# RWKV scan: four operands turned by 128x128 transposes for two chunks at a time, in place of 64x64 products with an identity

## The chip, the cores and the metric

One Trainium2 chip, and one of its cores. The time is the device time of one launch, in microseconds (us). Weights, inputs and constants lie in device memory; the kernel brings them in itself.

## The reference, cut to what matters

The program runs two transformer blocks after each other on 512 tokens of width 1024. The change lies in the second block, in its RWKV mixer, between the projections that make r, k, v, a, b and the output of the mixer:

```python
def rwkv7_scan(r, w, k, v, a, b):
    ...
    def step(state, inp):
        r_t, w_t, k_t, v_t, a_t, b_t = inp
        sa = jnp.einsum('bhvk,bhk->bhv', state, a_t)
        state = state * w_t[:, :, None, :] + sa[..., None] * b_t[:, :, None, :] + v_t[..., None] * k_t[:, :, None, :]
        return state, jnp.einsum('bhvk,bhk->bhv', state, r_t)
```

There are 16 heads of 64 features. The kernel does the recurrence in chunks of 64 tokens: within a chunk all 64 steps are written as products of 64x64 matrices per head, and a 64x64 state per head goes from chunk to chunk. All data is fp32.

## The kernel before, in words

The engines run their own programs, in the order in which a list of stages is built; semaphores tie them together. The stage of interest is `RwkvScan`. Ahead of it `RwkvInputs` makes the scaled operands r, k (`kx`), v, a (`aa`) and b (`bb`), each with the features on the partitions: tile p of 8 holds head 2p on partitions 0 to 63 and head 2p+1 on 64 to 127, and 512 tokens along the free axis. After it comes `SplitTiles` "gate_input", which splits the normalised input `xn` into a high and a low part (ScalarE writes `gate_input_hi`, GpSimd writes `gate_input_lo`), then `RwkvOutput` (norm, bonus, gate of the mixer), then `Gated` (projections).

`RwkvScan` goes over 8 chunks (`NCH`), c = 0 to 7, with a lead-in c = -1. In each turn of the loop the work of chunk c ("now") is woven with the first half of chunk c+1 ("next"): x, b_ra, d2, d2t, d4, d2_dm, d8, m2, m3 are "next", the others are "now". Each step is one `product`: 16 matmuls of 64x64 by 64x64, two per tile p, one for each head, with one PSUM bank as output; y has three such terms and z two. A `twin` (k_ra, b_ra, d2_dm) is 16 matmuls with 128 columns and fills two banks. The bonus is one full 128x128 matmul with 512 columns. Four products a chunk have the identity on the right: vn, bn, an, kn turn v, b, a and k of the chunk, so that tokens lie on the partitions; they are read as left factors by q, y and z (vn), z (bn, kn) and wt (an). (mn and mn2 use the identity too; the change leaves them.)

Each step takes the next of five PSUM banks in the order of the table `PERIOD`; a step can begin when the step five places before it has been drained (`open_aux`). TensorE signals `aux_full`; ScalarE copies most steps to SBUF (`copy`, L1994), VectorE drains the others: masks, sums (`summed`, L2046), the sum of sa (L2096) and of the state z (L2102, L2105), the bonus (L2080). Both work through their steps in program order. `state_ready` counts the state's updates, and `wait_end` waits for the last.

While RwkvInputs worked, the room of `xn` held its temporaries. `Move` "xn_back" brings `xn` back from device memory: one transfer of 2 MB that GpSimd issues (L2423), and for which `SplitTiles` "gate_input" waits on ScalarE (L514). On ScalarE the eight instructions of gate_input_hi stand before the squares of RwkvOutput (L2171):

```python
        load_xn = Move(k, "xn_back", xn, xn_dram, [inp.wait_scaled])
        scan = RwkvScan(k, inp, sbuf, ra)
        begin_gated = Begin(k)
        xs6 = SplitTiles(k, "gate_input", xn, view_r("gate_input_hi", 0, [DT_, S]),
                         view_r("gate_input_lo", 24576, [DT_, S]),
                         lambda e, j: (scan.wait_end(e), load_xn.wait_done(e)), alone=True)
        outp = RwkvOutput(k, scan, zg, inp.zg_ready, rr, vv, aa, kk,
                          view(30272, [DT_, S]))
```

Of the kernel before, what the change touches and what calls it, by code (L numbers as in the profile page):

```python
# [23 lines left out]
ACT = mybir.ActivationFunctionType  # L24
# [3 lines left out]
P = 128  # L28
S = 512
D = 1024  # L30
DT_ = D // P
# [1814 lines left out]
class RwkvScan(Stage):  # L1846
# [3 lines left out]

    PERIOD = (("next", "x"), ("now", "vn"), ("now", "k_ra0"), ("now", "k_ra1"), ("now", "mn"), ("now", "g"),
              ("next", "b_ra0"), ("next", "b_ra1"), ("now", "m4"), ("next", "d2"), ("next", "d2t"), ("now", "bn"),
              ("now", "g2"), ("now", "mn2"), ("next", "d4"), ("now", "an"), ("now", "bonus"), ("next", "d2_dm0"), ("next", "d2_dm1"),
              ("now", "m5"), ("now", "q"), ("next", "d8"), ("next", "m2"), ("now", "wt"), ("now", "u"), ("now", "kn"),
              ("now", "sa"), ("next", "m3"), ("now", "y"), ("now", "z"))

    def __init__(self, k, prep, buf, ra):

        super().__init__(k)
        self.prep, self.buf, self.ra = prep, buf, ra
        self.t = [{} for _ in range(NCH)]
        for c in range(-1, NCH):
            for which, step in self.PERIOD:
                at = c if which == "now" else c + 1
                if 0 <= at < NCH:
                    self.t[at][step] = k.take_aux()
        self.state_ready = k.sem("scan_state_ready")
        self.one_plus_d = k.sem("scan_one_plus_d_ready")  # L1870
        self.rkk_ready = k.sem("scan_rkk_ready")

    def chunk(self, ap, c):
        return ap[:, :, c * CH:(c + 1) * CH]

    def tensor(self, pe):
        k, b = self.k, self.buf
# [20 lines left out]
        def twin(t, name, lhs, rhs):  # L1898

            for half in range(2):  # L1900
# [6 lines left out]
                        mm = pe.matmul(out[part, p - 4 * half], lhs[part, p, :], rhs(p)[part], start=True, stop=True)  # L1907
                mm.then_inc(k.aux_full, 1)

        def drained(t, *steps):  # L1910

            for step in steps:
                k.wait_aux_drained(pe, t[step])

        for c in range(-1, NCH):
            n = c + 1
            now, nxt = c >= 0, n < NCH
            if now:
                t = self.t[c]
                ac, bc, kc, rc, vc = (self.chunk(x, c) for x in (aa, bb, kx, r, v))  # L1920
                x32, x64, rbt = b["x32"][c % 2], b["x64"][c % 2], b["rbt"][c % 2]
                ra = lambda p, c=c: self.ra[:, :, p * S + c * CH:p * S + (c + 1) * CH]
            if nxt:
                tn = self.t[n]
                an_, bn_ = self.chunk(aa, n), self.chunk(bb, n)
                ra_n = lambda p, n=n: self.ra[:, :, p * S + n * CH:p * S + (n + 1) * CH]
                product(tn["x"], (an_, bn_))
            if now:
                product(t["vn"], (vc, None))
                twin(t, "k_ra", kc, ra)  # L1930
                drained(t, "m3")
                product(t["mn"], (b["ml1"], None))
                product(t["g"], (x32, b["ml1"]))
            if nxt:
                twin(tn, "b_ra", bn_, ra_n)
            if now:
                drained(t, "mn", "g")
                product(t["m4"], (b["mn"], b["g"]))
            if nxt:
                drained(tn, "x", "b_ra0", "b_ra1")  # L1940
                product(tn["d2"], (b["dt"], b["d"]))
                product(tn["d2t"], (b["d"], b["dt"]))
            if now:
                product(t["bn"], (bc, None))
# [12 lines left out]
            if nxt:  # L1957
                pe.wait_ge(self.one_plus_d, n + 1)
                twin(tn, "d2_dm", b["d2"], lambda p: b["d2t_me0"][:, :, p, :])
            if now:  # L1960
                drained(t, "mn2", "g2")
                product(t["m5"], (b["mn"], b["g"]))
                drained(t, "k_ra0", "k_ra1", "vn")
                product(t["q"], (b["akt"], b["vn"]))
            if nxt:
                drained(tn, "d4", "d2_dm0", "d2_dm1")
                product(tn["d8"], (b["d4t"], b["d4"]))
                product(tn["m2"], (b["d4"], b["me1"]))
            if now:
                drained(t, "an", "m5")  # L1970
                product(t["wt"], (b["an"], b["ml1"]))
                drained(t, "q")
                product(t["u"], (b["ml1"], b["q"]))
                product(t["kn"], (kc, None))
                drained(t, "wt")
                pe.wait_ge(self.state_ready, c + 1)
                product(t["sa"], (b["wt"], b["z"]))
            if nxt:
                drained(tn, "d8", "m2")
                product(tn["m3"], (b["d8"], b["me0"]))  # L1980
            if now:
                drained(t, "sa")
                product(t["y"], (b["z"], rc), (b["sa"], rbt), (b["vn"], b["rkt"]))
                drained(t, "bn", "kn")
                product(t["z"], (b["bn"], b["sa"]), (b["kn"], b["vn"]))

    def scalar(self, act):


        k, b = self.k, self.buf  # L1990

        def copy(t, dst):
            k.wait_aux_full(act, t)
            act.activation(dst, k.aux(t).rearrange("p (a b) -> p a b", b=CH), ACT.Copy).then_inc(  # L1994
                k.aux_drained[t % NX], 1)

        for c in range(-1, NCH):
            now, nxt = c >= 0, c + 1 < NCH
            if now:
                t = self.t[c]  # L2000
                copy(t["vn"], b["vn"])
                copy(t["mn"], b["mn"])
                copy(t["g"], b["g"])
            if nxt:
                tn = self.t[c + 1]
                copy(tn["d2"], b["d2"])
                copy(tn["d2t"], b["d2t"])
            if now:
                copy(t["bn"], b["bn"])
                copy(t["g2"], b["g"])  # L2010
                copy(t["mn2"], b["mn"])
            if nxt:
                copy(tn["d4"], b["d4"])
            if now:
                copy(t["an"], b["an"])
                copy(t["q"], b["q"])
            if nxt:
                copy(tn["d8"], b["d8"])
            if now:
                copy(t["wt"], b["wt"])  # L2020
                copy(t["u"], b["u"])
                copy(t["kn"], b["kn"])
                copy(t["y"], self.chunk(self.prep.rkv[0], c))

    def vector(self, dve):
# [22 lines left out]
        for c in range(-1, NCH):  # L2048
# [430 lines left out]
def build(nc, x, consts, vecs, weights, bucket, rel, rel_last, mem, lora_in, out):  # L2479
    with ExitStack() as ctx:  # L2480
# [131 lines left out]
        for at, (name, n) in zip((38464, 38472, 38480, 38488, 38496), (("w0h", 8), ("a0h", 8), ("kah", 8), ("kac", 8), ("mu1", 27))):  # L2612
# [8 lines left out]
        names = ("x32", "x32", "x64", "x64", "rbt", "rbt", "d2", "d4", "d2t", "me0", "me1", "ml0", "ml1", "an", "q",  # L2621
                 "akt", "mn", "g", "vn", "bn", "kn", "rkt", "rkk", "d", "dt")
        sbuf = dict(zip(names, place))
        for i, n in enumerate(("x32", "x64", "rbt")):
            sbuf[n] = place[2 * i:2 * i + 2]
        for n, shared in (("d8", "d"), ("d4t", "dt"), ("wt", "akt"), ("u", "mn"), ("sa", "g")):
            sbuf[n] = sbuf[shared]
        sbuf["z"] = view(28672, [DT_, CH])
# [285 lines left out]
```

## Time and profile before

| what | value |
|---|---|
| time, median of 3 runs | 2407.27 us (2407.03 to 2411.24) |
| profiled execution, its own time | 2410.71 us |
| its span in the profile | 2408.8 us |
| TensorE matmul busy | 2217.2 us, 92% of the span |
| VectorE / ScalarE / GpSimd busy | 1043.4 / 870.9 / 333.1 us |
| matmuls of `product` (L1894), first and last start | 823.6 to 1081.6 us |

The profile is of one execution. Times in it count from the start of the span; "PE" is TensorE's matmuls, "PEld" its weight loads, DVE VectorE, ACT ScalarE, POOL GpSimd. The trace has two records for each fp32 matmul, so a product of 16 matmuls is "x32"; a transpose has one. The profiled execution's own time is 1.9 us above its span, and 3.4 us above the median of the runs.

### The profile page before, as it was taken

The numbers are of one execution on the slowest core, as the hardware profiler recorded it, in microseconds if no ns is written. First come the engines' busy times: TensorE is split into PE (matmuls) and PEld (weight loads), VectorE is DVE, ScalarE is ACT, GpSimd is POOL, SyncE is SP. The second block draws the span as 40 slices with busy tenths as digits, with TensorE's granted clock in tenths as the row PEclk, the third lists the DMA queues.
The fourth block names the chain that finished last, engine by engine and source line by source line (L and its number), as shares of the span: only waits on it lengthen the run. The fifth ranks groups of instructions, "written<-read, shape, count | busy, mean of one in ns | idle before, by whom it ended". The sixth has DMA issues, their size and how long they took to land.

```text
span 2408.8 us, 37512 instructions
## 1 busy us (share of the span) xinstructions
PE 2217.2 (92%) x16140; PEld 1682.4 (70%) x16140; DVE 1043.4 (43%) x1684; ACT 870.9 (36%) x1442; POOL 333.1 (14%) x395
## 2 busy tenths in 40 slices
PE   6988999999699899997999899979998787999999
PEld 3856788888366699992776664548776555888887
DVE  3144544343535544437334345563333444555522
ACT  3253333232445333334235136652243433333221
POOL 1443000001104200002000016660101012000000
PEclk8998999999899999997998799999998898999999
DMA  3212222232222200000253330002422101222222
GB/s 133 68 45 70 88 96 88 96 97 96 106 74 77 79 4 4 4 4 29 88 143 124 117 96 19 1 8 91 147 84 91 53 27 61 92 92 96 93 95 85
DMA packets 47411, 178.20 MB, mean 74 GB/s; under 512 B 5343, under 2 KB 5855, under 8 KB 46352
## 3 DMA queue, kind: packets, MB, share of 16 engines
q1 hardware_dynamic: 43056, 154.12, 19.4%
q0 software_dynamic: 4192, 21.70, 2.9%
q8 instruction: 128, 2.10, 0.4%
q14 instruction: 35, 0.29, 0.0%
HBM read 166.30 MB, written 10.55 MB: 73 GB/s over the span
## 4 chain that ended last, share of the span: by engine, by line
PE 82%; DVE 8%; ACT 5%; issue 3%; POOL 1%; DMA 1%; SPq 0%; DVEq 0%; ACTq 0%; POOLq 0%
PE ps L289 18%; PE ps L290 18%; PE ps L294 17%; PE ps L1894 8%; PE ps L474 4%; PE ps L1141 2%; PE ps L891 2%; PE ps L1907 2%; DVE arena L427 2%; PE ps L875 1%; PE ps L463 1%; PE ps L844 1%; ACT arena L986 1%; PE ps L408 1%; DVE arena L947 1%
## 5 line engine op out<-in xcount | busy, mean ns | idle before, releaser
L275 DVE TENSOR_TENSOR w_lo<-wring,w_hi 128x1024 fp32r<-128x1024 f32 (+1 forms) x243 | 301.9, 1244 | 340.1 <-ACT w_hi L269 340.1
L269 ACT ACTIVATE w_hi<-wring 128x1024 fp32r<-128x1024 f32 (+1 forms) x243 | 253.7, 1044 | 445.3 <-PE ps L294 430.9
L289 PE MATMUL ps<-ffn_input_hi,w_hi 128*128 128x512 f32 x352 | 141.8, 403 | 10.7 <-ACT ffn_input_hi L514 8.7
L290 PE MATMUL ps<-ffn_input_hi,w_lo 128*128 128x512 f32 x352 | 140.7, 400 | 0.0
L1894 PE MATMUL ps<-arena 64*64 64x64 f32 x4096 | 135.2, 218 | 5.3 <-issue 4.4
L1994 ACT ACTIVATE arena<-ps 128x512 f32<-128x512 f32 x120 | 71.7, 597 | 177.0 <-PE ps L1894 177.0
L1894 PEld LDWEIGHTS ps<-arena 64*64 64x64 f32 x4096 | 129.8, 135 | 7.4 <-issue 5.8
L1033 POOL TENSOR_TENSOR arena<-arena 128x512 f32<-128x512 f32 (+3 forms) x160 | 111.4, 721 | 39.2 <-DVE arena L939 34.2
L289 PE MATMUL ps<-mlp_input_hi,w_hi 128*128 128x512 f32 x256 | 102.9, 402 | 9.4 <-ACT mlp_input_hi L514 8.6
L641 DVE TENSOR_TENSOR arena<-arena,ps 128x512 f32<-128x512 f32 x56 | 38.5, 688 | 153.6 <-PE ps L294 153.6
L290 PE MATMUL ps<-mlp_input_hi,w_lo 128*128 128x512 f32 x256 | 102.1, 399 | 0.0
L289 PE MATMUL ps<-mlp_hi,w_hi 128*128 128x512 f32 x256 | 101.2, 395 | 0.0
L290 PE MATMUL ps<-mlp_hi,w_lo 128*128 128x512 f32 x256 | 101.2, 395 | 0.0
L986 ACT ACTIVATE arena<-arena 128x512 f32<-128x512 f32 (+3 forms) x160 | 88.2, 552 | 29.3 <-DVE arena L931 29.2
L289 PE MATMUL ps<-mixer_input_hi,w_hi 128*128 128x512 f32 (+1 forms) x216 | 90.6, 419 | 7.2 <-ACT mixer_input_hi L514 7.2
L474 PEld LDWEIGHTS ps<-wring,arena 128*128 128x128 f32 x832 | 96.0, 196 | 1.1 <-issue 1.0
L474 PE MATMUL ps<-wring,arena 128*128 128x128 f32 (+1 forms) x832 | 96.0, 279 | 0.0
L418 POOL TENSOR_TENSOR square<-square 128x512 f32<-128x512 f32 x21 | 36.4, 1735 | 412.2 <-ACT square L390 412.2
L294 PE MATMUL ps<-ffn_input_lo,w_hi 128*128 128x512 f32 x352 | 90.0, 397 | 0.1
L289 PEld LDWEIGHTS ps<-ffn_input_hi,w_hi 128*128 128x128 f32 x352 | 67.1, 191 | 30.9 <-issue 11.0
L289 PE MATMUL ps<-gate_input_hi,w_hi 128*128 128x512 f32 x192 | 79.7, 415 | 8.8 <-DVE w_lo L275 7.3
L290 PE MATMUL ps<-mixer_input_hi,w_lo 128*128 128x512 f32 (+1 forms) x216 | 87.6, 406 | 0.0
(358 smaller groups left out, 4545.1 us busy)
## 6 DMA issues: line engine op xcount, KB each, us to landing
wring<-weights SPq DMA_DIRECT2D x276, 512.0 KB, 3.3
bias_wide_scratch<-bias_line_scratch POOLq DMA_DIRECT2D x1, 4096.0 KB, 25.9
arena<-bias_wide_scratch POOLq DMA_DIRECT2D x1, 4096.0 KB, 16.9
wring<-weights SPq DMA_DIRECT2D x8, 384.0 KB, 3.0
arena<-x_t SPq DMA_DIRECT2D x1, 2048.0 KB, 7.7
x_scratch<-arena POOLq DMA_DIRECT2D x1, 2048.0 KB, 7.8
xn_scratch<-arena POOLq DMA_DIRECT2D x1, 2048.0 KB, 6.5
arena<-xn_scratch POOLq DMA_DIRECT2D x1, 2048.0 KB, 9.0
```

What stands on the lines that cost most here:

```text
L269: act.activation(self.w_hi[:, m % SPLIT, 0:n], self.wring[:, g % RING, 0:n], ACT.Copy).then_inc(self.w_hi_ready, 1)
L275: dve.tensor_tensor(self.w_lo[:, m % SPLIT, 0:n], self.wring[:, g % RING, 0:n], self.w_hi[:, m % SPLIT, 0:n].bitcast(F32), ALU.subtract).t ...
L289: pe.matmul(out, hi[:, c, :], src.hi[:, at + c, :], start=(at + c == 0), stop=False)
L290: pe.matmul(out, lo[:, c, :], src.hi[:, at + c, :], start=False, stop=False)
L294: mm = pe.matmul(out, hi[:, c, :], src.lo[:, at + c, :], start=False, stop=(last and c == kc - 1))
L427: dve.scalar_tensor_tensor(self.dst[:, j, :], self.src[:, j, :], k.vec(self.gain, j), r, ALU.mult, ALU.mult).then_inc(k.xn_ready, 1)
L474: mm = pe.matmul(k.acc(t)[:, b * self.m:(b + 1) * self.m], self.src(c)[:, b * P:(b + 1) * P], w[:, c, :], start=(c == 0), stop=(c == total ...
L891: mm = pe.matmul(out[e * HD:(e + 1) * HD, j * P:S], h.values(j, e), self.b.pt[e][:, COL[j]:COL[j] + S - j * P], start=(h.first and h.compr ...
L986: ins = act.activation(seg, seg, ACT.Exp, bias=b.negmax[:, u % 2, c], scale=-1.0, accum_out=b.sum[:, u % 2, c])
L1033: pool.tensor_tensor(seg, seg, inv[:, e:e + 1].to_broadcast([P, P * (i + 1)]), ALU.mult).then_inc(self.scaled, 1)
L1894: mm = pe.matmul(cut(out, p, e), cut(lhs, p, e), right, start=(i == 0), stop=(i == len(terms) - 1))
L1994: act.activation(dst, k.aux(t).rearrange("p (a b) -> p a b", b=CH), ACT.Copy).then_inc(k.aux_drained[t % NX], 1)
```

## The change

`turn` transposes v, b, k or a with `pe.transpose`: tile p of two chunks is 128 features by 128 tokens and is turned in one 128x128 transpose, so that chunk c comes to lie on partitions 0 to 63 and chunk c+1 on 64 to 127. Four tiles fill a bank, so a turn is 8 transposes and two banks (T0, T1). `turns` says for how many chunks a turn in chunk c is: v and b are turned in chunks 0, 2, 4, 6, for two chunks each; k and a in chunks 1, 3, 5 for two, and in chunks 0 and 7 for one (then 64 tokens wide). In the other chunks nothing is turned. That is 14 turns for two chunks and 4 for one.

The result has to be moved so that head 2p+e lies on partitions 64e to 64e+63. `turned` does that by copies of 64 partitions by 256 elements, two for each chunk and bank: ScalarE takes both banks of v and the first of b, a and k; VectorE the second of b, a and k. Each operand has two buffers by chunk parity. They lie in the room of `xn` (from 4096), so `xn_back` now waits for the end of the scan too.

```diff
+    def turns(self, name, c):
+        if name in "vb":
+            return (0, 2)[c % 2 == 0]
+        return 1 if c in (0, NCH - 1) else (0, 2)[c % 2]
+
+    def turned(self, eng, copy, name, c, half):
+        k = self.k
+        if self.turns(name, c):
+            t = self.t[c][f"{name}T{half}"]
+            k.wait_aux_full(eng, t)
+            for h in range(self.turns(name, c)):
+                x = k.aux(t)[h * CH:(h + 1) * CH, :].rearrange("p (a e b) -> p a e b", e=2, b=HD)
+                for e in range(2):
+                    dst = self.buf[f"{name}n"][(c + h) % 2][e * CH:(e + 1) * CH, 4 * half:4 * half + 4, :]
+                    ins = copy(dst, x[:, :, e, :])
+            ins.then_inc(k.aux_drained[t % NX], 1)
...
+        def turn(name, x, c):
+            width = CH * self.turns(name, c)
+            for half in range(2 if width else 0):
+                bank = self.t[c][f"{name}T{half}"]
+                k.open_aux(pe, bank)
+                for p in range(4):
+                    mm = pe.transpose(k.aux(bank)[0:width, p * P:(p + 1) * P],
+                                      x[:, 4 * half + p, c * CH:c * CH + width], k.const("ident"))
+                mm.then_inc(k.aux_full, 1)
...
-                product(t["vn"], (vc, None))
+                turn("v", v, c)
...
-                product(t["bn"], (bc, None))
+                turn("b", bb, c)
...
-                product(t["an"], (ac, None))
+                turn("a", aa, c)
...
-                product(t["kn"], (kc, None))
+                turn("k", kx, c)
...
-                copy(t["vn"], b["vn"])
+                self.turned(act, move, "v", c, 0)
+                self.turned(act, move, "v", c, 1)
...
-                copy(t["kn"], b["kn"])
+                self.turned(act, move, "k", c, 0)
...
                 summed(t["m4"], "ml0", "ml1", t["m3"])
+                self.turned(dve, dve.tensor_copy, "b", c, 1)
                 self.weigh(dve, c)
-                k.wait_aux_drained(dve, t["vn"])
+                self.turned(dve, dve.tensor_copy, "a", c, 1)
+                self.wait_turned(dve, "v", c)
...
             if now:
+                self.turned(dve, dve.tensor_copy, "k", c, 1)
                 k.wait_aux_drained(dve, t["u"])
                 k.wait_aux_full(dve, t["sa"])
...
-        load_xn = Move(k, "xn_back", xn, xn_dram, [inp.wait_scaled])
         scan = RwkvScan(k, inp, sbuf, ra)
+        load_xn = Move(k, "xn_back", xn, xn_dram, [inp.wait_scaled, scan.wait_end])
```

TensorE, before, in chunk 1 from d2 and d2t (the first row) on; rows with `consts_sb` and 64x64 are bn, mn2, an and kn, L1955 is the bonus, L1907 the twin d2_dm:

```order
L1894 MATMUL ps<-square 64x64 x32
L1894 MATMUL ps<-consts_sb,arena 64x64 x16
L1894 MATMUL ps<-arena 64x64 x16
L1894 MATMUL ps<-consts_sb,arena 64x64 x16
L1894 MATMUL ps<-arena 64x64 x16
L1894 MATMUL ps<-consts_sb,arena 64x64 x16
L1955 MATMUL ps<-arena,consts_sb 128x512
L1907 MATMUL ps<-arena 64x128 x16
L1894 MATMUL ps<-arena 64x64 x32
L1894 MATMUL ps<-arena,square 64x64 x16
L1894 MATMUL ps<-arena 64x64 x48
L1894 MATMUL ps<-consts_sb,arena 64x64 x16
```

TensorE now, in the same chunk, from m4, d2, d2t and g2 (the first row) on; L1942 are the transposes, of a and then of k:

```order
L1919 MATMUL ps<-arena 64x64 x64
L1919 MATMUL ps<-consts_sb,arena 64x64 x16
L1919 MATMUL ps<-arena 64x64 x16
L1942 MATMUL ps<-consts_sb,arena 128x128 x8
L1992 MATMUL ps<-arena,consts_sb 128x512
L1932 MATMUL ps<-arena 64x128 x16
L1919 MATMUL ps<-arena 64x64 x96
L1942 MATMUL ps<-consts_sb,arena 128x128 x8
L1919 MATMUL ps<-arena 64x64 x128
```

The turn of b between d2t and g2 is gone from this odd chunk; a, for two chunks, stands right ahead of the bonus, and k between u and sa.

VectorE, before, in chunk 1: the end of d2_dm (L2087), the sums of m5 and m2 (L2046), of sa (L2096), of m3, and the state:

```order
L2087 TENSOR_TENSOR arena<-arena,ps 128x256
L2046 TENSOR_TENSOR arena<-arena,ps 128x512 [waits aux_full,aux_drained4]
L2046 TENSOR_TENSOR arena<-arena,ps 128x512 [waits aux_full,aux_drained4,aux_drained3]
L2096 TENSOR_TENSOR arena<-arena,ps 128x512 [waits aux_full,aux_drained0]
L2046 TENSOR_TENSOR arena<-arena,ps 128x512 [waits aux_full,aux_drained3]
L2102 TENSOR_TENSOR arena<-arena,ps 128x512 [waits scan_state_ready,aux_full]
```

VectorE now, at the same place:

```order
L2131 TENSOR_TENSOR arena<-arena,ps 128x256
L2088 TENSOR_TENSOR arena<-arena,ps 128x512 [waits aux_full,aux_drained2]
L2088 TENSOR_TENSOR arena<-arena,ps 128x512 [waits aux_full,aux_drained2,aux_drained1]
L1892 COPY arena<-ps 64x256 [waits aux_full]
L1892 COPY arena<-ps 64x256 x3
L2141 TENSOR_TENSOR arena<-arena,ps 128x512 [waits aux_full,aux_drained3]
L2088 TENSOR_TENSOR arena<-arena,ps 128x512 [waits aux_full,aux_drained1]
L2147 TENSOR_TENSOR arena<-arena,ps 128x512 [waits scan_state_ready,aux_full]
```

Four copies of k now stand between the sum of m2 and the sum of sa.

GpSimd, around the scan (L1841 and L1843 are the last work of RwkvInputs, L1325 belongs to a later stage), as a difference, with the semaphores waited for:

```order
 L1841 TENSOR_TENSOR arena<-arena 128x512 [waits kk_a_ready]
 L1843 TENSOR_TENSOR arena<-arena 128x512 [waits acc_drained2]
-L2423 DMA arena<-xn_scratch 128x4096 [waits bkr_scaled_ready,a_scaled_ready]
+L2468 DMA arena<-xn_scratch 128x4096 [waits scan_state_ready,bkr_scaled_ready,a_scaled_ready]
 L518 TENSOR_TENSOR gate_input_lo<-arena,gate_input_hi 128x512 [waits gate_input_hi_ready] x8
-L1325 DMA arena<-rel_bias 32x16 [waits aux_drained4]
+L1325 DMA arena<-rel_bias 32x16 [waits aux_drained3]
```

The order is the same; the transfer has one more semaphore to wait for, that of the scan's state.

## Rows read from the trace of the kernel before

**Rows 1.** The page's first line

```profile
span 2408.8 us, 37512 instructions
```

**Rows 2.** Windows: the scan's middle; busy us (records) by engine, PEclk the granted clock

```profile
855.00:1050.00 195.00, 194.28 (x5782) 188.08 (x5783) 84.84 (x163) 58.55 (x99) 0.00 (x0) 1.00 0.02 4
```

**Rows 3.** Timeline in chunk 1: start, us, engine, line, xcount

```profile
880.71 1.13 PE L1894 MATMUL ps<-consts_sb,arena 64*64 64x64 f32 x32
881.64 1.13 PE L1894 MATMUL ps<-arena 64*64 64x64 f32 x32
...
884.44 1.13 PE L1894 MATMUL ps<-consts_sb,arena 64*64 64x64 f32 x32
885.50 1.12 PE L1955 MATMUL ps<-arena,consts_sb 128*128 128x512 f32 x2
886.56 1.96 PE L1907 MATMUL ps<-arena 64*64 64x128 f32 x32
```

**Rows 4.** Chain that ended last, behind the scan: a full fp32 matmul of 512 columns

```profile
1093.60 0.86 PE ps L2155 x2
```

**Rows 5.** Timeline of TensorE in the attention: transposes (L875) between 64-row products

```profile
1486.61 0.88 PE L875 MATMUL ps<-consts_sb,arena 128*128 128x128 f32 x6
1487.41 0.70 PE L844 MATMUL ps<-arena 64*128 64x256 f32 x4
```

**Rows 6.** Transposes: duration ns min/median/max; then a run of eight (start, us)

```profile
L875 PE MATMUL ps<-consts_sb,arena x400: 272/273/332, 147.5 to 1603.6; 128*128 128x128 f32 x134
1933.64 1.09 PE L2253 MATMUL ps<-consts_sb,arena 128*128 128x128 f32 x8 [2.31 <-DVE arena L2285]
```

**Rows 7.** Timeline of TensorE in the last chunk: m4, bn, g2

```profile
1063.91 1.15 PE L1894 MATMUL ps<-arena 64*64 64x64 f32 x32 [0.73 <-issue]
1064.87 1.13 PE L1894 MATMUL ps<-consts_sb,arena 64*64 64x64 f32 x32
1065.91 1.15 PE L1894 MATMUL ps<-arena 64*64 64x64 f32 x32
```

**Rows 8.** Groups by form: copies out of PSUM; busy us, mean ns

```profile
L1159 ACT ACTIVATE arena<-ps 128x256 f32<-128x256 f32 x8 | 3.1, 384 | 19.7 <-PE ps L1141 19.3
L1000 ACT ACTIVATE arena<-ps 64x512 f32<-64x512 f32 x8 | 4.6, 574 | 0.0
L2086 DVE COPY square<-ps 128x256 f32<-128x256 f32 x16 | 6.8, 424 | 7.2 <-PE ps L1907 6.8
```

**Rows 9.** Timeline in chunk 1, second half: sa, m3 (their weight loads), sum of sa, y

```profile
894.83 1.02 PEld L1894 LDWEIGHTS ps<-arena 64*64 64x64 f32 x32
895.76 1.02 PEld L1894 LDWEIGHTS ps<-arena,square 64*64 64x64 f32 x32
896.11 0.69 DVE L2096 TENSOR_TENSOR arena<-arena,ps 128x512 f32<-128x512 f32 x1 [3.02 <-PE ps L1894]
896.85 5.72 PEld L1894 LDWEIGHTS ps<-arena 64*64 64x64 f32 x190
```

**Rows 10.** DMA issues: KB each, median us from issue to landing

```profile
arena<-x_t SPq DMA_DIRECT2D x1, 2048.0 KB, 7.7
arena<-xn_scratch POOLq DMA_DIRECT2D x1, 2048.0 KB, 9.0
arena<-mem_t POOLq DMA_DIRECT2D x1, 1024.0 KB, 11.8
```

**Rows 11.** Timeline at the end of the scan

```profile
1083.30 4.27 ACT L514 ACTIVATE gate_input_hi<-arena 128x512 fp32r<-128x512 f32 x8 [1.77 <-DVE arena L2105]
1087.47 1.13 ACT L2171 ACTIVATE square<-arena 128x512 f32<-128x512 f32 x2
1088.23 1.63 PE L2155 MATMUL ps<-square,consts_sb 128*128 128x512 f32 x2 [4.50 <-ACT square L2171]
```

**Rows 12.** Windows: clock in the attention, and just behind the scan (columns as in group 2)

```profile
1479.70:1500.00 20.30, 18.95 (x131) 10.36 (x130) 12.24 (x54) 13.56 (x43) 13.54 (x26) 1.00 0.00 1
1089.00:1091.00 2.00, 2.00 (x4) 0.80 (x3) 0.69 (x1) 0.00 (x0) 2.00 (x3) 0.50 0.00 0
```

More of the change, by code:

```diff
@@ L1846 @@
 class RwkvScan(Stage):
[L1853 to L1856, printed above, removed]
+    PERIOD = (("next", "x"), ("now", "vT0"), ("now", "vT1"), ("now", "k_ra0"), ("now", "k_ra1"), ("now", "mn"), ("now", "g"),
+              ("next", "b_ra0"), ("next", "b_ra1"), ("now", "m4"), ("next", "d2"), ("next", "d2t"), ("now", "bT0"), ("now", "bT1"),
+              ("now", "g2"), ("now", "mn2"), ("next", "d4"), ("now", "aT0"), ("now", "aT1"), ("now", "bonus"), ("next", "d2_dm0"), ("next", "d2_dm1"),
+              ("now", "m5"), ("now", "q"), ("next", "d8"), ("next", "m2"), ("now", "wt"), ("now", "u"), ("now", "kT0"), ("now", "kT1"),
               ("now", "sa"), ("next", "m3"), ("now", "y"), ("now", "z"))
@@ L1866, in __init__ @@
                 at = c if which == "now" else c + 1
-                if 0 <= at < NCH:
+                if 0 <= at < NCH and (step[1:2] != "T" or self.turns(step[0], at)):
                     self.t[at][step] = k.take_aux()
@@ L1874, in chunk, with wait_turned @@
         return ap[:, :, c * CH:(c + 1) * CH]
+    def turns(self, name, c):
[13 more added lines that the diff above has]
+            ins.then_inc(k.aux_drained[t % NX], 1)
+    def wait_turned(self, eng, name, c):
+        start = next(i for i in range(c, -1, -1) if self.turns(name, i))
+        for half in range(2):
+            self.k.wait_aux_drained(eng, self.t[start][f"{name}T{half}"])
     def tensor(self, pe):
@@ L1919, in tensor @@
                 t = self.t[c]
-                ac, bc, kc, rc, vc = (self.chunk(x, c) for x in (aa, bb, kx, r, v))
+                kc, rc = self.chunk(kx, c), self.chunk(r, c)
+                vn, bn, kn, an = (b[f"{name}n"][c % 2] for name in "vbka")
                 x32, x64, rbt = b["x32"][c % 2], b["x64"][c % 2], b["rbt"][c % 2]
@@ L1962, in tensor @@
                 product(t["m5"], (b["mn"], b["g"]))
-                drained(t, "k_ra0", "k_ra1", "vn")
-                product(t["q"], (b["akt"], b["vn"]))
+                drained(t, "k_ra0", "k_ra1")
+                self.wait_turned(pe, "v", c)
+                product(t["q"], (b["akt"], vn))
             if nxt:
@@ L1969, in tensor @@
             if now:
-                drained(t, "an", "m5")
-                product(t["wt"], (b["an"], b["ml1"]))
+                drained(t, "m5")
+                self.wait_turned(pe, "a", c)
+                product(t["wt"], (an, b["ml1"]))
                 drained(t, "q")
                 product(t["u"], (b["ml1"], b["q"]))
-                product(t["kn"], (kc, None))
+                turn("k", kx, c)
                 drained(t, "wt")
@@ L1982, in tensor @@
                 drained(t, "sa")
-                product(t["y"], (b["z"], rc), (b["sa"], rbt), (b["vn"], b["rkt"]))
-                drained(t, "bn", "kn")
-                product(t["z"], (b["bn"], b["sa"]), (b["kn"], b["vn"]))
+                product(t["y"], (b["z"], rc), (b["sa"], rbt), (vn, b["rkt"]))
+                self.wait_turned(pe, "b", c)
+                self.wait_turned(pe, "k", c)
+                product(t["z"], (bn, b["sa"]), (kn, vn))
     def scalar(self, act):
@@ L1995, in copy @@
                 k.aux_drained[t % NX], 1)
+        move = lambda dst, src: act.activation(dst, src, ACT.Copy)
         for c in range(-1, NCH):
@@ L2008, in scalar @@
             if now:
-                copy(t["bn"], b["bn"])
+                self.turned(act, move, "b", c, 0)
                 copy(t["g2"], b["g"])
@@ L2014, in scalar @@
             if now:
-                copy(t["an"], b["an"])
+                self.turned(act, move, "a", c, 0)
                 copy(t["q"], b["q"])
@@ L2620, in build @@
         place += [k.square[:, i, :].rearrange("p (a b) -> p a b", b=CH) for i in range(4)]
-        names = ("x32", "x32", "x64", "x64", "rbt", "rbt", "d2", "d4", "d2t", "me0", "me1", "ml0", "ml1", "an", "q",
-                 "akt", "mn", "g", "vn", "bn", "kn", "rkt", "rkk", "d", "dt")
+        names = ("x32", "x32", "x64", "x64", "rbt", "rbt", "d2", "d4", "d2t", "me0", "me1", "ml0", "ml1", "q",
+                 "akt", "mn", "g", "rkt", "rkk", "d", "dt")
         sbuf = dict(zip(names, place))
@@ L2627, in build @@
             sbuf[n] = sbuf[shared]
+        spare = [view(4096 + S * i, [DT_, CH]) for i in range(8)]
+        for i, n in enumerate("vbka"):
+            sbuf[f"{n}n"] = spare[2 * i:2 * i + 2]
         sbuf["z"] = view(28672, [DT_, CH])
```

## The prediction

> **What bounds the kernel now.** I read the page first for the span the sum is made against [rows 1]; 1.9 us lie around it, and the profiled execution took 2410.71 us, 3.4 above the median of 2407.27. The scan is some 260 us of it. Then the windows: in the 195 us of its middle TensorE is busy 194.28, at a granted clock of 1.00, while VectorE has 84.84 and ScalarE 58.55 us of work [rows 2]. So the order of TensorE is the path there, and what is taken from it counts in full wherever no answer of another engine is due just then. The timeline gives the price of a step and shows where such answers are due; the end of the scan has to be read apart, because the change moves a transfer there.
>
> **What is removed.** Four products in each of 8 chunks, 32 in all. Four steps in a row take 884.44 - 880.71 = 3.73 us, so one is 0.933 [rows 3], and 32 are 29.9 us. One of them is not won: in the last chunk nothing of a next chunk lies between m4 and g2, and g2 has to wait for VectorE's sum of m4. m4 starts at 1063.91, bn at 1064.87, g2 only at 1065.91, 2.0 us after m4 [rows 7]; without bn that gap stays. I take 0.9 off: 29.0.
>
> **What TensorE gets instead.** 18 turns of 8 transposes. The attention has the same instruction in the same form. One alone lasts 273 ns, but eight in a row take 1.09, that is (1.09 - 0.27) / 7 = 0.117 each [rows 6]; a run of six goes from 1486.61 to the next matmul's start at 1487.41, 0.80, which is 6 x 0.117 and 0.10 more [rows 5]. A turn is so 8 x 0.117 = 0.94 us. Against 16 small matmuls for one chunk (0.933) this serves two.
>
> To that comes the change of shape: small products use a quarter of the array in two places, a transpose all of it. The bonus shows what it costs. The product ahead of it starts at 884.44 and would be through at 885.37, the bonus starts at 885.50: 0.13. From its start to the twin's are 1.06 us [rows 3], where the same amount of work at full clock takes 0.86 behind the scan [rows 4]: 0.20. So 0.33 for the way in and out. The run of six in the attention had only 0.10 for its one change [rows 5]; I take 0.33.
>
> v, b and k for two chunks: 11 turns at 1.27 = 14.0. The three of a for two chunks stand right ahead of the bonus, whose way in they take over: 3 x 0.94 = 2.8. Four turns for one chunk (k and a in chunks 0 and 7): 8 transposes each too. They have half the columns to load, but the same 128 to stream, and no row shows them, so I price them like the others: k 2 x 1.27, a 2 x 1.07 (a change of width ahead of the bonus), 4.7. Together 21.5. TensorE: -29.0 + 21.5 = -7.5 us.
>
> **The copies.** A copy of 512 elements becomes four of 256 elements on 64 partitions (two, where one chunk is turned). On ScalarE 256 elements from PSUM take 0.38, and 64 partitions are no cheaper than 128 (0.574 at 512 elements); on VectorE 256 take 0.42 [rows 8]. Where they lie:
> - v, 8 on ScalarE in even chunks, 3.1 us. The next thing it owes is mn. From the first bank's end to that of mn TensorE has half the turn, the twin k_ra and mn, about 0.7 + 1.8 + 0.9 = 3.4. Cost 0. If they took longer, two banks of v would come free late, and behind mn and g the twin b_ra opens the second of these.
> - b, 4 on VectorE in even chunks, 1.7, ahead of the two instructions that make the bonus' operand (0.69 each): 3.1. TensorE meanwhile has g2, mn2, d4 and the change of shape, 3.1, and in even chunks no turn of a behind. I take 0.1 x 4 = 0.4. Behind the bonus in TensorE's queue stands the twin d2_dm, for which VectorE waits, and m2 behind that.
> - k, 4 on VectorE in chunks 1, 3, 5, between the sum of m2 and the sum of sa. Now the sum starts 1.28 after sa's start and y 2.02 after it, once the sum has ended; m3 fills the time [rows 9]. The last transpose of k starts some 0.3 before sa; 0.34 later its bank is seen, and the copies end 1.4 to 1.7 us behind that, 0.1 to 0.4 past the time at which the sum could start. All of that reaches y: 0.27 x 3 = 0.8.
> - a, 4 on VectorE after these two instructions and ahead of the bonus, on an engine that waits there anyway: 0.
>
> Copies: 1.2. The scan: -7.5 + 1.2 = **-6.3 us**.
>
> **The transfer at the end.** Now xn_back leaves when RwkvInputs is done and has the whole scan to land; its 9.0 us from issue to landing [rows 10] cost nothing. This cover goes. On ScalarE gate_input_hi is the first thing behind the scan: it starts at 1083.30, released by the state's last instruction L2105, its eight take until 1087.5, then come the squares, and TensorE waits for these until 1088.23 (4.50 idle) [rows 11]. With the change GpSimd sees the last state, issues 2 MB, and ScalarE stands until they land. Queued behind that are its own squares, VectorE's variances, TensorE's products with them, and GpSimd's gate_input_lo. None has other work that is not already in the shadow of gate_input_hi. So 9.0 + 0.2 for GpSimd's wake-up = **+9.2 us**. Bounds: 7.7, the quickest read of 2 MB, and 11.8, the slowest read from GpSimd's queue [rows 10]; I keep to this transfer's own 9.0. The clock has already fallen to half behind the present wait (0.50 from 1089 [rows 12]), so a longer one does not buy a new fall.
>
> **Sum.** -6.3 + 9.2 = +2.9: the profiled execution would go from 2410.7 to 2413.6, the median from 2407.27 to **2410.2 us**, 0.12% more. A change of less than 0.2%, 4.8 us, cannot well be told from none.
>
> **The rivals.**
> - *The array takes longer to empty for a whole-array step than the bonus shows* (slower). For it: a turn's two banks are signalled apart, and the bonus has only one matmul to load behind the change. Against it: the attention's 0.10. 13 turns pay it in full and 2 the way in; at twice the price it is 4.6 more, 2414.8. It decides from 1.9 us on, 0.14 us a turn. Chance 0.22.
> - *The turns that are 64 wide go as ordinary fp32 matmuls.* 512 columns take 0.86 [rows 4], so 128 take 0.215, a turn 1.72 in place of 0.94: +3.1 for four, 2413.3. Against it: nothing but the width differs from the others. Chance 0.08. The Trainium skill speaks for it: "TensorEngine Tiling (Array Packing)", section "Tile-to-Partition Mapping", says that column tiling switches off the transpose mode for fp32 input. No row shown has so narrow a transpose.
> - *Transposes let the clock fall.* A turn at half clock would take twice its time: 18 x 0.94 = 17 more, 2427. Against it: the 20.3 us of the attention that hold the run of six run at 1.00 [rows 12]. Chance 0.03. The Trainium skill, "TensorE: Matmul & The Clock Gate", section "Part 4: PE-mode transpose", says that transposes don't count as activity in the way that matmuls do; this trace gives no sign of it in a mixed stream.
> - *Weight loads hide behind the transposes, and the change of shape is nearly free* (faster). Then a transpose is its 128 columns alone, about half of 0.117: 144 x 0.058 = 8.4 less, and up to 4.6 for the change of shape, at the best 2397; half of it, 2403.7, is not yet faster. Against it: eight in a row already show 0.117. The transfer at 7.7 would add 1.3. Chance 0.13.
> - *The transfer takes longer than 11 us* because weights are fetched beside it: 2412.4. Only 4 GB/s moved in the scan's middle [rows 2], and the ring is full. Chance 0.03.
>
> **How the numbers follow.** The forecast with its own scatter (switch 0.2 to 0.45, transpose 0.11 to 0.13, copies 0 to 3, transfer 8.5 to 10) runs from 2404 to 2412 and has the remaining 0.51. So within 0.2% has 0.51, slower 0.36, faster 0.13. The range of 8 in 10 reaches into both neighbours: down to 2402, up to 2417, leaving out the clock rival, the ends of the others.
>
> **What would show it.** In the scan: 18 runs of 8 one-record transposes, 0.94 each from first start to the end of streaming, with 0.13 ahead and 0.20 behind; a pair of chunks (1 and 2, say) 7.46 us of products less and 5.1 of turns and copies more, 2.3 shorter; y in chunks 1, 3, 5 a few tenths later behind m3. If the scan gets shorter by far more or less than 6, the price of a turn is wrong. At its end: ScalarE idle for about 9 us with the transfer of xn as what ends it, and TensorE idle some 14. If gate_input_hi starts within 5 us of the state's end, the second term is wrong, and the kernel comes out faster.

## The result

| kernel | median of its runs | ratio to before, 95% interval |
|---|---|---|
| before | 2407.31 us (2405.00 to 2411.24, 20 runs) | |
| changed | 2411.48 us (2409.25 to 2415.39, 19 runs) | 1.0016 [1.0009, 1.0023] |

The changed kernel is 4.2 us, 0.16% by the ratio, slower: less than 0.2%, and for all that not zero. A twentieth run was disturbed (3175 us) and is left out. Its profiled execution took 2409.97 us.

The page of the changed kernel, its head and the first table (engine, busy us, share, instructions):

```profile
span 2408.0 us, 35864 instructions
PE 2203.4 (92%) x15260; PEld 1666.8 (69%) x15260; DVE 1063.0 (44%) x1732; ACT 881.4 (37%) x1490; POOL 332.7 (14%) x395
```

The line of the transposes (L1942), with least, median and longest ns of one:

```profile
L1942 PE MATMUL ps<-consts_sb,arena x144: 272/273/331, 837.5 to 1065.5; 128*128 128x128 f32 x112, 128*64 128x128 f32 x32
```

144 of them, one record each, the 64 wide ones too.

The timeline of chunks 1 and 2, the places where the new instructions stand:

```profile
880.69 1.09 PE L1942 MATMUL ps<-consts_sb,arena 128*128 128x128 f32 x8
881.62 1.02 PE L1992 MATMUL ps<-arena,consts_sb 128*128 128x512 f32 x2
882.58 1.96 PE L1932 MATMUL ps<-arena 64*64 64x128 f32 x32
...
890.07 1.09 PE L1942 MATMUL ps<-consts_sb,arena 128*128 128x128 f32 x8
891.20 1.73 DVE L1892 COPY arena<-ps 64x256 f32<-64x256 f32 x4 [2.09 <-PE ps L1942]
892.96 0.69 DVE L2141 TENSOR_TENSOR arena<-arena,ps 128x512 f32<-128x512 f32 x1
893.70 5.98 PE L1919 MATMUL ps<-arena 64*64 64x64 f32 x192 [0.53 <-DVE arena L2141]
...
899.61 1.09 PE L1942 MATMUL ps<-consts_sb,arena 128*128 128x128 f32 x8
900.63 1.96 PE L1932 MATMUL ps<-arena 64*64 64x128 f32 x32
...
910.41 1.73 DVE L1892 COPY arena<-ps 64x256 f32<-64x256 f32 x4 [2.01 <-PE ps L1942]
912.17 0.69 DVE L2159 TENSOR_TENSOR arena<-arena 128x512 f32<-128x512 f32 x1
912.90 0.69 DVE L2160 TENSOR_TENSOR arena<-arena,vecs_sb 128x512 f32<-128x512 f32 x1
913.74 1.10 PE L1992 MATMUL ps<-arena,consts_sb 128*128 128x512 f32 x2 [0.42 <-DVE arena L2160]
...
943.21 1.53 PE L1932 MATMUL ps<-arena 64*64 64x128 f32 x24
```

A turn of v is 1.02 us from its start to the next start, one of a ahead of the bonus 0.93. But twice TensorE now stands for VectorE: 0.53 us, because the copies of k lie ahead of the sum of sa (L2141) that y reads, and 0.42, because the copies of b lie ahead of the two instructions (L2159, L2160) that make the bonus' operand. The last row is the twin d2_dm two chunks on, 60.63 us after that of 882.58. Before, the twin stands at 886.56 in [rows 3], and in the same timeline two chunks on at 949.26, which is 62.70:

```profile
949.26 1.42 PE L1907 MATMUL ps<-arena 64*64 64x128 f32 x22
```

So a pair of chunks is 2.07 us shorter.

The end of the scan in the timeline, to set beside [rows 11]:

```profile
1073.48 0.69 DVE L2150 TENSOR_TENSOR arena<-arena 128x512 f32<-128x512 f32 x1
1074.73 0.59 POOL L2468 DMA_DIRECT2D arena<-xn_scratch  x1 [254.78 <-DVE arena L2150]
1083.48 4.27 ACT L514 ACTIVATE gate_input_hi<-arena 128x512 fp32r<-128x512 f32 x8 [11.04 <-DMA arena<-xn_scratch]
1087.65 1.14 ACT L2216 ACTIVATE square<-arena 128x512 f32<-128x512 f32 x2
1088.41 2.04 PE L2200 MATMUL ps<-square,consts_sb 128*128 128x512 f32 x2 [13.77 <-ACT square L2216]
```

The last state instruction starts at 1073.48 and ScalarE's first tile at 1083.48, 10.00 later; before, the two were 0.73 apart. That is 9.3 us for the transfer. What follows the wait, from the chain of work that ended last:

```profile
1088.41 2.04 PE ps L2200 x2
1090.45 1.71 PE ps L2195 x2
1092.16 1.71 PE ps L2200 x2
1093.87 1.06 PE ps L2195 x2
```

Each piece is a product of two passes, which takes 0.86 at full clock. The same four pieces took 1.63, 1.71, 1.18 and 0.86 before: 1.1 us more are lost at half clock (granted 0.50 there, [rows 12]). How much of it the longer wait makes is seen only beside other versions (below).

The balance by trace: from the scan's first product to the last state instruction 253.42 us, 258.94 before, so -5.5; the transfer +9.3; the half clock +1.1. That makes +4.9 against 4.2 of the medians. It is a balance of these stretches and not of the whole: the two profiled executions have spans of 2408.0 and 2408.8 us. The changed kernel's scan starts 3.6 us earlier in it (820.06 for 823.63), ahead of anything that was changed, and 2.1 us more come back behind the four pieces. Both lie within the scatter of one kernel's runs (2405.00 to 2411.24 before). So the trace shows where the terms lie, and the medians what they come to.

### The profile page after: what moved, and what is told of

Its sections match the earlier page's. It is cut to its first block, busy times and chain, and to the rows that moved or that the text cites. A ratio compares the mean times of both kernels' runs of the same rounds, so it can differ in the third digit from the quotient of the medians.

```text
span 2408.0 us, 35864 instructions
## 1 busy us (share of the span) xinstructions
PE 2203.4 (92%) x15260; PEld 1666.8 (69%) x15260; DVE 1063.0 (44%) x1732; ACT 881.4 (37%) x1490; POOL 332.7 (14%) x395
## 4 chain that ended last, share of the span: by engine, by line
PE 81%; DVE 9%; ACT 5%; issue 3%; DMA 1%; POOL 1%; SPq 0%; DVEq 0%; ACTq 0%; POOLq 0%
PE ps L289 18%; PE ps L290 17%; PE ps L294 17%; PE ps L1919 6%; PE ps L474 4%; PE ps L1141 2%; PE ps L891 2%; PE ps L1932 2%; DVE arena L427 2%; PE ps L875 1%; PE ps L463 1%; PE ps L844 1%; ACT arena L986 1%; PE ps L408 1%; DVE arena L947 1%
## 5 line engine op out<-in xcount | busy, mean ns | idle before, releaser
L1919 PE MATMUL ps<-arena 64*64 64x64 f32 x5120 | 163.4, 219 | 11.7 <-issue 5.3
L1919 PEld LDWEIGHTS ps<-arena 64*64 64x64 f32 x5120 | 157.9, 135 | 17.1 <-issue 12.7
L2034 ACT ACTIVATE arena<-ps 128x512 f32<-128x512 f32 x96 | 57.3, 597 | 153.4 <-PE ps L1919 153.3
```

The costliest lines, as they stand in the source:

```text
L1919: mm = pe.matmul(cut(out, p, e), cut(lhs, p, e), right, start=(i == 0), stop=(i == len(terms) - 1))
```

## The experiments

All times are medians of runs against the kernel before on the same chip (2407.3 to 2408.5 us there). All versions compute the same outputs.

### The transfer alone: `xn_late`

The kernel before, products and all, with its transfer behind the scan:

```diff
-        load_xn = Move(k, "xn_back", xn, xn_dram, [inp.wait_scaled])
         scan = RwkvScan(k, inp, sbuf, ra)
+        load_xn = Move(k, "xn_back", xn, xn_dram, [inp.wait_scaled, scan.wait_end])
```

> The kernel before with one edit: xn_back waits for the end of the scan too; the scan itself is untouched. Theory A (the two terms of the prediction: the turns win some 6 us, the late transfer costs some 9 to 10): 9.2 to 11 us slower than before, ratio 1.004 to 1.0045, with gate_input_hi 9 to 10 us after the state's last instruction. Rival B (the transfer is mostly hidden by work that ScalarE or TensorE find meanwhile, and what ate the gain is in the turns): less than 4 us slower, below 1.0017.

Measured: 2417.87 us, ratio 1.0044 [1.0031, 1.0056], 10.0 us over the kernel before. The timeline has the same gap of 11 us on ScalarE:

```profile
1083.80 0.59 POOL L2423 DMA_DIRECT2D arena<-xn_scratch  x1 [260.45 <-DVE arena L2105]
1092.56 4.27 ACT L514 ACTIVATE gate_input_hi<-arena 128x512 fp32r<-128x512 f32 x8 [11.06 <-DMA arena<-xn_scratch]
1097.49 2.04 PE L2155 MATMUL ps<-square,consts_sb 128*128 128x512 f32 x2 [13.79 <-ACT square L2171]
```

So the wait costs its full length: ScalarE's first tile starts 10.01 us behind the last state instruction (1082.55), 9.3 more than in the kernel before. The four pieces at the clock's change take 5.97 us for 5.38, so another 0.6 at half clock; together 9.9 of the measured 10.0. The rival by which the transfer is partly hidden falls.

### The scan alone: `roomy`

The changed kernel with room elsewhere for the turned operands, so that `xn_back` can leave early again:

```diff
-        spare = [view(4096 + S * i, [DT_, CH]) for i in range(8)]
+        spare = place[21:27] + [view(37952, [DT_, CH]), k.root[:, :].rearrange("p (a b) -> p a b", b=CH)]
...
+        load_xn = Move(k, "xn_back", xn, xn_dram, [inp.wait_scaled])
         scan = RwkvScan(k, inp, sbuf, ra)
-        load_xn = Move(k, "xn_back", xn, xn_dram, [inp.wait_scaled, scan.wait_end])
```

> The changed kernel with the eight turned buffers in other room (six that the scan had left over, one behind them, one in the tile of the roots), so that xn_back leaves ahead of the scan as it did before. Theory A: the scan's gain alone, 5 to 6.5 us faster than before, ratio 0.9973 to 0.9979. Rival B: within 2 us of before, 0.999 to 1.001.

Measured: 2401.85 us, ratio 0.9975 [0.9966, 0.9984], 6.1 less than before. Together with `xn_late` (+10.0) this gives +3.9, and the full change +4.2: the two terms add up. TensorE's wait for the squares is 4.50 us here, as before, yet the four pieces behind it take 5.93 us for 5.38:

```profile
1078.65 2.04 PE ps L2200 x2
1080.70 1.71 PE ps L2195 x2
1082.40 1.32 PE ps L2200 x2
1083.72 0.86 PE ps L2195 x2
```

So half of the 1.1 us of half clock in the changed kernel is there without the long wait.

### VectorE's order: `roomy_order`

`roomy`, with the copies of b behind `weigh` and those of k behind the sum of sa:

```diff
-                self.turned(dve, dve.tensor_copy, "b", c, 1)
                 self.weigh(dve, c)
+                self.turned(dve, dve.tensor_copy, "b", c, 1)
...
-                self.turned(dve, dve.tensor_copy, "k", c, 1)
                 k.wait_aux_drained(dve, t["u"])
                 k.wait_aux_full(dve, t["sa"])
                 done(dve.tensor_tensor(row(b["sa"]), row(b["u"]), k.aux(t["sa"]), ALU.add), t["sa"])
+                self.turned(dve, dve.tensor_copy, "k", c, 1)
```

> As roomy, and on VectorE the copies of k stand behind the sum of sa, those of b behind the two instructions that make the bonus' operand. In the trace of the changed kernel TensorE stood 0.53 us ahead of y in chunks 1, 3, 5 and 0.42 ahead of the bonus in chunks 2, 4, 6. If these waits come from the place of the copies, they go: some 2.5 us less than roomy (3 x 0.4 and 3 x 0.4 above what was there before). Rival: the copies delay whatever stands behind them (the sum of m3, the state, d2_dm), and the time is that of roomy.

Measured: 2397.89 us, ratio 0.9959 [0.9945, 0.9973], 10.0 under before and 4.0 under `roomy`: the right sign, more than expected. The chain of `roomy` behind the turn of k in chunk 1:

```profile
889.62 1.04 PE ps L1942 x8
...
892.44 0.70 DVE arena L2141
...
893.18 5.98 PE ps L1919 x192
899.16 1.02 PE ps L1942 x8
```

and that of `roomy_order` at the same place:

```profile
891.96 1.02 PE ps L1942 x8
892.98 7.92 PE ps L1919 x256
900.90 1.02 PE ps L1942 x8
```

From the turn of k to the next of v are 9.54 us in the one, 8.94 in the other; from the turn of b to the bonus 4.39 and 3.97. A pair of chunks is 1.06 shorter (59.57 for 60.63), three pairs 3.2. The rest, 1.0, is a stall in the lead-in, ahead of the first of these copies; `roomy` has it and `roomy_order` has not (last section).

### The width of a turn: `one_chunk`

`roomy`, with every operand turned in every chunk, 32 turns of 64 tokens:

```diff
-        if name in "vb":
-            return (0, 2)[c % 2 == 0]
-        return 1 if c in (0, NCH - 1) else (0, 2)[c % 2]
+        return 1
```

> As roomy, with every turn for one chunk: 32 turns 64 tokens wide in place of 18, two copies a bank in place of four. If a turn costs the same 0.94 us and its changes of shape whatever its width (theory A), 14 more turns at 1.1 to 1.2 make it 14 to 17 us slower than roomy, and 9 to 11 slower than before. Rival C (a 64-wide transpose costs half of a 128-wide one): 32 turns at about 0.7 are 22, so about as fast as roomy. Rival D (narrow transposes run as ordinary fp32 matmuls): 32 turns at 1.9 or more, over 30 us slower than before.

Measured: 2412.99 us, ratio 1.0015 [1.0006, 1.0024], 4.5 over the kernel before and so 10.5 over `roomy`: theory A has the right side and misses both of its ranges (14 to 17, 9 to 11). The line of its transposes:

```profile
L1940 PE MATMUL ps<-consts_sb,arena x256: 272/273/302, 840.0 to 1078.7; 128*64 128x128 f32 x128
```

One record each, and eight in 0.99 us to the next start, where 128 wide ones take 1.02. So half the width saves next to nothing. By trace the scan is 10.7 us longer than in `roomy` (264.05 for 253.39). In `roomy` 2.9 us of it are waits for VectorE's copies (three times 0.53 and 0.42), and here, with two copies a bank, these waits are gone, which the forecast left out. The 14 turns more are so some 13.5 us, 0.97 each. The rival by which narrow ones run as ordinary fp32 matmuls (over 30 more here) falls. The Trainium skill, "TensorEngine Tiling (Array Packing)", section "Tile-to-Partition Mapping", would have had it so, if a transpose 64 wide counts as column tiling; this trace doesn't agree: 128*64 transposes have one record and the rate of the others.

### Transposes or products: `plain_matmul`

`roomy`, with the turns as ordinary fp32 matmuls by the 128x128 identity:

```diff
-                    mm = pe.transpose(k.aux(bank)[0:width, p * P:(p + 1) * P],
-                                      x[:, 4 * half + p, c * CH:c * CH + width], k.const("ident"))
+                    mm = pe.matmul(k.aux(bank)[0:width, p * P:(p + 1) * P], x[:, 4 * half + p, c * CH:c * CH + width],
+                                   k.const("ident"), start=True, stop=True)
```

> As roomy, with the 144 transposes written as ordinary matmuls with the 128x128 identity on the right. By the full fp32 matmul of 512 columns (0.86 us) one of 128 columns takes 0.215 and more, a transpose 0.117: 14 to 17 us slower than roomy, two records each. If the rate of a turn is set by its weight loads and not by passes over the columns, it is less than 7 us slower.

Measured: 2418.31 us, ratio 1.0047 [1.0034, 1.0061], 9.8 over the kernel before and so 15.9 over `roomy`, in the range of 14 to 17. The line has 288 records for the same 144 instructions, two passes each; a turn of k takes 1.99 us to the next start for 1.02, and the scan 17.4 us more than in `roomy`. The rival by which the weight loads set the rate falls. What the change wins in the scan hangs on the transpose's single pass.

### The split moved: `split_later`, `before_split_later`, `best`

In all versions so far ScalarE's squares stand behind gate_input_hi. Here they come first: in the changed kernel, in the kernel before, and in `roomy_order` (that one is called `best`, which it was not).

```diff
+        outp = RwkvOutput(k, scan, zg, inp.zg_ready, rr, vv, aa, kk,
+                          view(30272, [DT_, S]))
         xs6 = SplitTiles(k, "gate_input", xn, view_r("gate_input_hi", 0, [DT_, S]),
                          view_r("gate_input_lo", 24576, [DT_, S]),
                          lambda e, j: (scan.wait_end(e), load_xn.wait_done(e)), alone=True)
-        outp = RwkvOutput(k, scan, zg, inp.zg_ready, rr, vv, aa, kk,
-                          view(30272, [DT_, S]))
```

> The changed kernel, xn_back as late as in it, with the stage that splits xn (gate_input) built behind RwkvOutput: ScalarE does its squares and logarithms first, gate_input_hi after them. If the transfer costs time only because ScalarE stands at it with its squares queued behind, then the 9.8 us go, and the 4.3 us of the eight instructions too: 12 to 15 us faster than the changed kernel, 8 to 11 faster than before, ratio 0.9955 to 0.9967. Rival: Gated waits for gate_input_lo, which GpSimd begins some 30 us later, and half or more of it comes back.

> The kernel before with one edit: the gate_input split stands behind RwkvOutput. xn has landed long ago, so what can go is the 4.3 us in which ScalarE splits ahead of its squares: 3 to 5 us faster than before, 0.998 to 0.9988, unless GpSimd's part comes too late for Gated (then no faster).

> roomy_order and the later gate_input split together: 8 us (scan) and 4 us (split) less than before, 2395 to 2397, ratio 0.9945 to 0.9960. If split_later shows that Gated waits, less.

Measured: `split_later` 2404.67, ratio 0.9988 [0.9979, 0.9996]; `before_split_later` 2410.95, 1.0007 [0.9998, 1.0016]; `best` 2400.97, 0.9966 [0.9955, 0.9978]. All three miss: the first wins 3.2 us on before and not 8 to 11 (about 7 on the changed kernel and not 12 to 15), the second nothing, and the third is some 3 us behind `roomy_order`. The transfer itself is hidden in the first: TensorE waits 2.08 us for its squares, as in the other two. The timeline of `before_split_later` shows why:

```profile
1110.90 1.85 DVE L2202 SCALAR_TENSOR_TENSOR arena<-arena,vecs_sb 128x512 f32<-128x512 f32 x1
1110.95 12.98 POOL L518 TENSOR_TENSOR gate_input_lo<-arena,gate_input_hi 128x512 fp32r<-128x512 f32 x8 [286.95 <-ACT gate_input_hi L514]
1112.79 1.65 DVE L2203 SCALAR_TENSOR_TENSOR arena<-arena,vecs_sb 128x512 f32<-128x512 f32 x1
1114.47 0.69 DVE L2206 TENSOR_TENSOR arena<-arena,ps 128x512 f32<-128x512 f32 x1
...
1134.40 2.07 PE L2161 MATMUL ps<-arena,wring 128*128 128x512 f32 x2 [3.09 <-DVE arena L2206]
```

The same instructions in the kernel before, whose GpSimd was done with its eight tiles (10.10 us for them) at 1094.1:

```profile
1115.66 0.75 DVE L2202 SCALAR_TENSOR_TENSOR arena<-arena,vecs_sb 128x512 f32<-128x512 f32 x1
1117.23 0.69 DVE L2206 TENSOR_TENSOR arena<-arena,ps 128x512 f32<-128x512 f32 x1
```

Counted from the last state instruction, VectorE's scalings (L2202, L2203) come 4.1 us earlier (28.95 for 33.09). But beside GpSimd they take 1.03 to 1.85 us for 0.75, the first eight 11.5 us in place of 6.0; GpSimd's tiles take 1.62 for 1.26. L2206, with one operand in PSUM, keeps its 0.69. TensorE gets the second half late (3.09 us idle), and the first product of Gated, 55.4 us behind the last state instruction before, starts 56.5 behind it: the gain is gone. ScalarE's part of the split also runs there, but it is through at 1114.5, and the scalings are long up to 1124, where GpSimd ends.

### The split between the squares: `before_woven`, `woven`

If only instructions with two operands in SBUF suffer, the split belongs beside VectorE's subtraction of the mean, which reads PSUM. In the kernel before and in `roomy_order`:

```diff
             act.activation(k.square[:, p % 4, :], self.y[:, p, :], ACT.Square).then_inc(k.square_ready, 1)
+            for j in ((), (0, 1, 2), (3,), (4,), (5,), (6,), (7,), ())[p]:
+                self.split.tile(act, j)
```

> The kernel before, with one edit: the eight instructions of gate_input_hi stand between the squares on ScalarE (three behind the second square, one behind each of the next five), and no longer ahead of all squares. So GpSimd's gate_input_lo runs beside VectorE's subtractions of the mean, which read PSUM and one SBUF operand, and not beside the scalings, which read two operands in SBUF. Theory A (only VectorE instructions with two SBUF operands stretch beside GpSimd's): the subtractions stay near 0.69 us, the scalings at 0.75, GpSimd's eight tiles take little over 10.1, and TensorE's first product with squares comes 4.27 us earlier: 4 to 5 us under the kernel before, ratio 0.9979 to 0.9983. Rival B (any VectorE instruction stretches beside GpSimd's): the subtractions take 1.2 to 1.8 us and the chain over eight tiles gets as much longer as it was moved forward, gain under 1 us. Rival C (the instructions between the squares hold up the squares themselves): each pair of tiles takes 0.5 us more, gain 1 to 2 us. If the idle time of TensorE ahead of the squares falls from 4.5 us to near nothing, the half clock behind it may go too, another 1 to 2 us.

> The version with its own room for the turned operands, the early transfer and the reordered copies (measured 2397.89 us, ratio 0.9959), with the eight instructions of gate_input_hi between the squares. By theory A of the run beside it the two gains add up: 2392 to 2394.5 us, ratio 0.9935 to 0.9945. By B or C of that run it stays at 2396 to 2398, ratio 0.9950 to 0.9960.

Measured: `before_woven` 2404.27, ratio 0.9984 [0.9975, 0.9993]; `woven` 2393.65, 0.9943 [0.9930, 0.9957]. The timeline of `before_woven` (L523 is GpSimd's split, L2192 the subtraction, L2209 the first of the two scalings):

```profile
1084.58 6.20 POOL L523 TENSOR_TENSOR gate_input_lo<-arena,gate_input_hi 128x512 fp32r<-128x512 f32 x5 [262.22 <-ACT gate_input_hi L515]
...
1085.59 0.69 DVE L2192 TENSOR_TENSOR arena<-arena,ps 128x512 f32<-128x512 f32 x1 [0.24 <-PE ps L2155]
...
1109.25 0.75 DVE L2209 SCALAR_TENSOR_TENSOR arena<-arena,vecs_sb 128x512 f32<-128x512 f32 x1
```

Nothing stretches: the subtraction stays at 0.69, the tiles at 1.24 to 1.27, the scalings at 0.75. From the last state instruction to the first scaling are 28.96 us (1080.29 to 1109.25), 33.09 before (1082.57 to 1115.66): 4.1 won.

That this is near the 4.27 that stood in the way is luck. TensorE's first product with squares starts 3.23 us behind the last state instruction, 5.66 before, so only 2.4 earlier; the chain shows what the squares wait for now, VectorE's part of a weight (`w_lo`) and its subtraction:

```profile
1080.98 1.14 DVE w_lo L275
1082.11 0.61 DVE arena L2192
1082.74 0.64 ACT square L2176
```

The other 1.7 are the clock: with TensorE idle for 2.08 us in place of 4.50 the four pieces take 3.68 us for 5.38. The rivals, by which everything stretches or the squares are held up by the split, fall. `woven` is the fastest version of this study, 13.8 us under before and 18 under the change as it was made.

## Why the prediction came out

It said 2410.2 us, 2.9 over before; it is 4.2 over. Step by step:

- **What is removed, what TensorE gets.** The right mechanism, priced too dear. The turns of a pair of chunks were put at 3 x 1.27 + 0.94 = 4.75. A turn is 1.02 to the next start, of which 0.09 are the way out (0.20 was said). For the way in k shows 0.10: the six products ahead of it start at 884.37, would be through after 6 x 0.933 at 889.97, and it starts at 890.07. So 1.12, three of them and one of a (0.93) are 4.3. 64 wide turns cost as much as the others, as the forecast had them. Worked out in this way the 18 turns are some 19 us, where 21.5 was said.
- **The copies.** The right places, the wrong size. k delays y by 0.53 (0.27 was said), b the bonus by 0.42 (0.1 was said). A pair: -7.46 of products, +4.3 and +0.95 of waits make -2.2, near the measured -2.07, where -2.3 was forecast. In all these waits are 2.9 us, where 1.2 was said for the copies. That they are the path is shown: `roomy_order` takes them away and is 1.06 us a pair shorter.
- **The scan.** -6.3 was said. From the first turned operand on (837.50 now, vn at 839.94 before) to the last state instruction it is 235.98 for 242.63, -6.65. The whole scan has -5.5, since its lead-in is 1.1 longer (below). That the first figure is so near is in part luck: turns 2.4 too dear and copies 1.7 too cheap cancel for the most part.
- **The transfer.** +9.2 was said, +9.3 by the trace. Of its parts the wake-up was put too short (it is 0.56 from the state's end, 1074.17, to GpSimd's start, and not 0.2) and the landing too long (8.7 us for 9.0).
- **The clock.** This term was put at nothing, because the clock is down already behind the wait of 4.50. It isn't nothing: the four pieces take 1.1 us more than before. Two comparisons differ in the transfer (the second also in where the turned operands lie), and both give 0.6 for it: `xn_late` 5.97 for 5.38 before, the changed kernel 6.52 for 5.93 in `roomy`. The other 0.5 comes with the same wait of 4.50 and is not explained. Each figure is from one execution.

The rivals: emptying of the array is not dearer but cheaper. Narrow turns as ordinary matmuls: refuted by `one_chunk`. The clock doesn't fall in transposes: from 855 to 1050 us the granted clock is 1.00 with them too, and eight take 1.09 us as in [rows 6]. Weight loads hidden behind the transposes: no, 0.117 each stands. The transfer over 11 us: no. By trace the error is 2.0 us (+4.9 for +2.9): 1.1 of clock, 1.1 of lead-in and 0.1 of transfer, less the 0.4 by which the rest of the scan came out better; the medians have 1.3 of it.

## What to carry to other kernels

Ask of every freed or borrowed piece of memory which early transfer it holds back: here a faster scan paid for a wait that other free room avoids, and `roomy` turns +4.2 into -6.1 with the same engine code in the scan. Put copies that nobody waits for behind the instruction that somebody does: four of 0.42 us ahead of it held TensorE up by about half a microsecond each time, and the two places of a pair cost nearly as much as one turn. And before work of GpSimd is moved, look at which operands VectorE reads at the place where it comes to lie.

## What was unexpected of the hardware

- **GpSimd and VectorE.** VectorE's instructions with two SBUF operands took 1.03 to 1.85 us for 0.75 beside a GpSimd subtraction that reads SBUF, and that took 1.62 a tile for 1.26; those with one operand in PSUM kept 0.69. The Trainium skill, "SBUF — State Buffer", section "Who interferes with whom", says just this, that a VectorE instruction with two SBUF inputs contends with a GpSimd instruction that reads SBUF, and that one with at most one does not; the traces of `before_split_later` and `before_woven` agree.
- **The clock behind a wait.** The length of TensorE's wait doesn't tell alone what is lost at half clock. The first four pieces took 6.52 us (the changed kernel) and 5.97 (`xn_late`) behind 13.8 us idle. Behind 4.50 us they took 5.38 (before), 5.93 (`roomy`), 5.31 (`roomy_order`) and 5.37 (`one_chunk` and `plain_matmul`); in the last two the first piece still has nearly full speed, 1.16 and 1.14 us, and the second has 1.71. Behind 2.08 us, in the five versions with the squares first or woven, they took 3.68, the speed of the pieces further on.
- **A stall in the lead-in.** The first two steps of the scan are the same instructions in all versions, yet in the changed kernel, `split_later`, `roomy`, `one_chunk` and `plain_matmul` the twin b_ra takes some 3.5 us, and in the other seven profiles 1.94 or 1.95. It makes the next product 0.8 to 1.0 later. The timeline of `roomy`:

```profile
819.60 1.35 PE L1919 MATMUL ps<-arena 64*64 64x64 f32 x32 [2.95 <-issue]
...
820.68 3.46 PE L1932 MATMUL ps<-arena 64*64 64x128 f32 x32
```

and of `roomy_order`, whose TensorE program is the same:

```profile
822.89 1.15 PE L1919 MATMUL ps<-arena 64*64 64x64 f32 x32 [2.95 <-issue]
...
823.84 1.94 PE L1932 MATMUL ps<-arena 64*64 64x128 f32 x32
```

No wait is recorded inside the twin. The stall does not follow the time at which the scan starts (819.60 or 822.63, the same stall). The five versions that have it are those with turns and with VectorE's copies in their first order; the versions with products, and those with the copies moved, don't have it. Yet no such copy runs so early, and each version has one trace only. `split_later` has a delay of the same kind once more: from the product at 1057.00 to the turn of a 3.50 us for 2.02 in the changed kernel. No run here tells what makes it, and it stays open.
